# Strassen products of the feed-forward part in the order 1, 5, 7, 6, 2, 3, 4 instead of 1, 5, 6, 7, 3, 2, 4

## The chip, the cores and the metric

The kernel runs on one core of a Trainium2 chip. The metric is the device time of one execution in microseconds. TensorE (PE) multiplies, VectorE (DVE), ScalarE (ACT) and GpSimd (POOL) work element by element, SyncE (SP) issues most of the transfers, and each runs its own instruction queue in order; semaphores tie them together.

## The reference

One step of a decoder trunk. Three token mixers and their gates come first; the change touches only the feed-forward part behind them, with D = 1024, D_FF = 2816 and 1056 rows (1024 of the prompt, 32 of the samples):

```
x = x + (mixed @ w_out).astype(x.dtype)
h2 = rmsnorm(x, norm2_w)
gu = h2 @ w_ffn_up
x = x + ((jax.nn.silu(gu[..., :D_FF]) * gu[..., D_FF:]) @ w_ffn_down).astype(x.dtype)
...
y_prompt = rmsnorm(xp, final_norm_w)
y_sample = rmsnorm(xs, final_norm_w)
```

## The kernel before

Every operand of a matmul is split into a high and a low part, so that each product of tiles takes three matmuls (low times high, high times low, high times high: L2144, L2145, L2146). The mixers and the output projection fill the first 1005 us. From there on the feed-forward part runs as 37 "pairs" x, each a 2 by 2 block product done in Strassen-Winograd form with seven block products instead of eight. Pairs 0 to 20 (`UP_PAIRS` = 21) make the up projection: one pair gives one tile of the gate half and one of the value half for all 1056 columns, in two halves of 528 (`LOWER`, `UPPER`). Pairs 21 to 36 make the down projection: four groups d of 4, 6, 6 and 6 tiles of the inner dimension (`DOWN_TILES`), and in each group four pairs m. A product is 24 matmuls of 264 columns in an up pair, 12 in group 0 and 18 in groups 1 to 3.

**Accumulators.** Four pairs of PSUM banks ("quads") hold the products. Products 1, 5, 7 and 2 start a quad afresh; 6 is added onto 1 in the same quad, 3 onto 5, and 4 onto 7 (`QUAD`, `FRESH`). So product 6 may start only when 1 has been read out, 3 when 5 has, and 4 when 7 has. The rule for that is `bank_free` (L2105): it waits on counters of the reading engines.

**Readers, up pair.** ACT copies quad 1 to R1 (L2696) once product 1 is done, and the sum 1+6 to R2 (L2708). DVE then makes RV = R2 + 5, f upper = RV + 7, f lower = R2 + 3, RG = R1 + 2, RV = R2 + 4 ("quadrants", L3300 and below, counter `dr`), ACT applies SiLU to RG and RV (L2674), and DVE multiplies them in (`ffn_product`). Beside every odd pair the operands for the down projection are made of two finished f tiles: DVE forms four sums, ACT casts seven high parts (`f_high`, L2669), DVE subtracts seven low parts (`f_low`), and SP stores them in HBM (L1125).

**Readers, down pair.** DVE adds the quads straight onto X1 (`down_add`, counter `dd`): one add for product 1 and 5 each, three for 1+6, one for 7, 3, 2, 4 each, nine in all. In the last three pairs the squares of the final norm are added between them (`square_sum`).

**Weights.** SP loads the raw weights of a pair (`raw_load`), ACT casts the high part of each product's stationary operand into a ring of six slots (`weight_high`, L2643), POOL subtracts the low part (`low`) and overwrites the raw tiles with the four weight differences that later products need (`difference`; both are L1249). All queues are written out by hand in the order of the products. `ORDER[i]` is the product at position i, and `done_count` the value of the matmul counter when it is done. The operands of the down projection come back from HBM by `f_load`, one per product and group, into tiles that `F_AT` names.

Lines that matter here:

```python
ORDER, LAST_ORDER = (1, 5, 6, 7, 3, 2, 4), (1, 5, 6, 7, 4, 3, 2)
QUAD = {1: 0, 6: 0, 5: 2, 3: 2, 7: 4, 4: 4, 2: 6}
...
    after(act, pd, done_count(x, 1))
    if x >= 1:
        after(act, dr, 5 * x - 1)
    nc.scalar.copy(by_chunk(R1), quad(1)).then_inc(ar_used.sem, 1)
```

## Time and profile before

| what | us |
|---|---|
| median of 3 runs | 1741.16 |
| lowest and highest | 1740.33, 1742.37 |
| the profiled execution's own time | 1742.4 |
| its span, first to last instruction | 1740.7 |
| PE busy with matmuls | 1660.2 (95%) |
| ACT, DVE, POOL busy | 557.6, 951.8, 797.6 |
| up pairs 0 to 20 | 1013.2 to 1471.1 |
| down pairs 21 to 36 and final norm | 1471.1 to 1740.7 |

The profile is of one execution; its own time lies 1.2 us above the median and 1.7 us above its span. Mean granted clock of TensorE over the span: 0.989 of full speed. In the views below, a row of the timeline gives start, duration, engine, line, operation, output and inputs, and in brackets how long the engine had been idle before it and what released it. A row of the waits gives the total, the number and the longest of such waits.

### The profile page before, as it was taken

Reading aid. Unit: us, or ns where it says so; the run is one execution under the profiler, and the core shown is the slowest. Engines: PE = TensorE matmul, PEld = TensorE weight load, DVE = VectorE, ACT = ScalarE, POOL = GpSimd, SP = SyncE. Lnnn points to the kernel's source line nnn. Section 1 sums busy time; section 2 is a strip of 40 time slices with the busy share of each in tenths; the row PEclk is TensorE's granted clock in tenths of the full one; section 3 lists DMA queues with packets and bytes.
Section 4 is the critical chain, followed back from the end, with each engine's and each line's share of the span. In section 5 each row is a group of like instructions: output and inputs, shape, how many; then the busy total and the mean of one; then the engine's idle time right before and its main releaser. Section 6 shows DMA issues by size and latency. Waiting matters only on the chain.

```text
span 1740.7 us, 30849 instructions
## 1 busy us (share of the span) xinstructions
PE 1660.2 (95%) x12229; PEld 1605.7 (92%) x12229; DVE 951.8 (55%) x1615; ACT 557.6 (32%) x1239; POOL 797.6 (46%) x761
## 2 busy tenths in 40 slices
PE   7999999999999999999999969999999999889995
PEld 7999999999999998788999969999999998889994
DVE  6859711407345546869742575555555554724446
ACT  5332121432123324434210343334333433312232
POOL 5482122222221121323322357777777775757772
PEclk9999999999999999999999989999999999999998
DMA  5454463232323246243552503333343347877432
GB/s 202 87 120 133 124 188 99 88 89 85 96 91 99 86 141 196 87 148 124 198 183 86 197 25 137 136 136 136 136 136 136 137 161 289 315 278 274 181 140 100
DMA packets 94299, 252.36 MB, mean 145 GB/s; under 512 B 14528, under 2 KB 35008, under 8 KB 93912
## 3 DMA queue, kind: packets, MB, share of 16 engines
q1 hardware_dynamic: 72144, 180.98, 30.8%
q10 hardware_dynamic: 12056, 37.03, 6.2%
q0 software_dynamic: 9968, 32.54, 6.1%
q8 instruction: 90, 1.47, 0.3%
q14 instruction: 41, 0.34, 0.1%
HBM read 179.85 MB, written 70.44 MB: 144 GB/s over the span
## 4 chain that ended last, share of the span: by engine, by line
PE 75%; DVE 8%; POOL 7%; issue 4%; ACT 4%; DMA 2%; SPq 0%; ACTq 0%; DVEq 0%; POOLq 0%
PE ps L1559 14%; PE ps L1560 13%; PE ps L1561 13%; PE ps L2144 9%; PE ps L2146 9%; PE ps L2145 9%; POOL RAWB L1249 4%; DVE X L2789 1%; POOL WL L1249 1%; DMA x_scratch<-X 1%; POOL RINGB L1249 1%; POOL WH L1249 1%; ACT STG L2669 1%; PE ps L1989 1%; PE ps L2080 1%
## 5 line engine op out<-in xcount | busy, mean ns | idle before, releaser
L1559 PE MATMUL ps<-HL,WH 128*128 128x384 f32 x1488 | 492.3, 331 | 5.3 <-DVE HL L685 1.8
L1560 PE MATMUL ps<-HH,WL 128*128 128x384 f32 x1488 | 481.7, 324 | 0.0
L1561 PE MATMUL ps<-HH,WH 128*128 128x384 f32 x1488 | 481.1, 323 | 0.0
L1559 PEld LDWEIGHTS ps<-HL,WH 128*128 128x128 f32 x1488 | 280.6, 189 | 16.7 <-issue 9.3
L1560 PEld LDWEIGHTS ps<-HH,WL 128*128 128x128 f32 x1488 | 280.8, 189 | 0.3
L1561 PEld LDWEIGHTS ps<-HH,WH 128*128 128x128 f32 x1488 | 280.5, 188 | 0.0
L1224 POOL TENSOR_TENSOR WL<-WRAW,WH 128x1024 fp32r<-128x1024 f32 x59 | 145.1, 2459 | 233.8 <-DMA WH<-in_w 233.8
L2789 DVE TENSOR_TENSOR X<-X,ps 128x528 f32<-128x528 f32 (+1 forms) x162 | 107.2, 681 | 177.0 <-PE ps L2146 126.1
L1221 POOL DMA_DIRECT2D WH<-in_w x59 | 34.5, 585 | 364.8 <-PE ps L1561 363.2
L2201 ACT ACTIVATE GT<-ps 128x384 f32<-128x384 f32 (+1 forms) x72 | 33.3, 464 | 214.9 <-PE ps L1561 183.8
L1249 POOL TENSOR_TENSOR RAWB<-RAWB 128x512 f32<-128x512 f32 (+2 forms) x76 | 98.5, 1297 | 7.2
L2144 PE MATMUL ps<-SOP,WH 128*128 128x264 f32 x268 | 78.1, 292 | 19.9 <-ACT FS L2648 9.0
L1249 POOL TENSOR_TENSOR WRAW<-WRAW 128x512 f32<-128x512 f32 (+2 forms) x72 | 86.7, 1204 | 6.8
L2144 PE MATMUL ps<-HL,WH 128*128 128x264 f32 x304 | 86.3, 284 | 3.3 <-issue 3.3
L2789 DVE TENSOR_TENSOR RB<-RB,ps 128x528 f32<-128x528 f32 x63 | 44.0, 699 | 81.8 <-ACT RB L2708 51.4
L2144 PE MATMUL ps<-SOP,WL 128*128 128x264 f32 x270 | 78.0, 289 | 8.2 <-ACT RB L2696 7.3
L2145 PE MATMUL ps<-HH,WL 128*128 128x264 f32 x292 | 83.1, 285 | 0.0
L2146 PE MATMUL ps<-HH,WL 128*128 128x264 f32 x292 | 83.0, 284 | 0.0
L2145 PE MATMUL ps<-HH,RINGB 128*128 128x264 f32 x292 | 82.9, 284 | 0.0
L2146 PE MATMUL ps<-HH,RINGB 128*128 128x264 f32 x292 | 82.8, 284 | 0.0
L2144 PE MATMUL ps<-SOP,RINGB 128*128 128x264 f32 x254 | 72.9, 287 | 7.3 <-ACT RB L2696 3.7
L2145 PE MATMUL ps<-HH,WH 128*128 128x264 f32 x280 | 79.6, 284 | 0.0
(459 smaller groups left out, 4301.2 us busy)
## 6 DMA issues: line engine op xcount, KB each, us to landing
WRAW<-in_w SPq DMA_DIRECT2D x75, 512.0 KB, 3.3
ffn_scratch<-STG SPq DMA_DIRECT2D x70, 528.0 KB, 4.0
WH<-in_w POOLq DMA_DIRECT2D x60, 512.0 KB, 4.5
SOP<-ffn_scratch SPq DMA_DIRECT2D x36, 528.0 KB, 12.9
gate_scratch<-GT ACTq DMA_DIRECT2D x24, 528.0 KB, 3.5
HH<-ffn_scratch SPq DMA_DIRECT2D x24, 528.0 KB, 9.0
PX<-gate_scratch ACTq DMA_DIRECT2D x22, 528.0 KB, 4.0
RAWB<-in_w SPq DMA_DIRECT2D x11, 1024.0 KB, 5.0
```

The costliest lines, as they stand in the source:

```text
L1221: nc.gpsimd.dma_start(WH[:, slot, 0:wd], src[:, 0:wd]).then_inc(s_high[slot], 16)
L1224: nc.gpsimd.tensor_tensor(WL[:, slot, 0:wd], WRAW[:, slot, 0:wd], WH[:, slot, 0:wd].bitcast(F32), ALU.subtract).then_inc(split_ok, 1)
L1249: return nc.gpsimd.tensor_tensor(out, a, b, op)
L1559: nc.tensor.matmul(out, wh, rl, start=start, stop=False)
L1560: nc.tensor.matmul(out, wl, rh, start=False, stop=False)
L1561: return nc.tensor.matmul(out, wh, rh, start=False, stop=stop)
L1989: last = nc.tensor.matmul(bank[3 + kv][:, 256 * i + lo:256 * i + 256], blk(PU[r:r + 64, 4 + 2 * half + i, :], n), PX[r:r + 64, 6, P * (n - ...
L2144: nc.tensor.matmul(out, wh, ml, start=product in FRESH and k == 0, stop=False, skip_group_check=True)
L2145: nc.tensor.matmul(out, wl, mh, start=False, stop=False, skip_group_check=True)
L2146: last = nc.tensor.matmul(out, wh, mh, start=False, stop=k == nk - 1, skip_group_check=True)
L2201: nc.scalar.activation(GT[:, c0:c0 + w], acc_of(no, n)[:, 0:w], ACT.Tanh, scale=0.5).then_inc(acc_free[n], 1)
L2789: return nc.vector.tensor_tensor(out, a, b, op)
```

## The change

The order of the products becomes 1, 5, 7, 6, 2, 3, 4 in all pairs but the last, and 1, 5, 7, 6, 4, 3, 2 in the last. Products 6 and 7 change places, and so do 3 and 2. Everything that is written in the order of the products is moved along: the counts that TensorE waits for, the order of low parts and differences on POOL, of casts and copies on ACT, and of quadrants and adds on DVE. On ACT the cast for the next pair's first product now stands ahead of the R2 copy, and two casts of the down operands stand one weight cast earlier. The tiles of group 0 and 1 of the down operands are permuted, so that each load still goes into a tile that is free by then; each product still reads its own operand from the HBM scratch (`ROW_OF`). Nothing is added or removed: the number of matmuls, element-wise operations and transfers and their sizes stay the same.

```diff
@@ -66,7 +66,7 @@
 UP_PAIRS = DFF // P - 1
 DOWN_TILES = [4, 6, 6, 6]
 PAIRS = UP_PAIRS + 4 * len(DOWN_TILES)
-ORDER, LAST_ORDER = (1, 5, 6, 7, 3, 2, 4), (1, 5, 6, 7, 4, 3, 2)
+ORDER, LAST_ORDER = (1, 5, 7, 6, 2, 3, 4), (1, 5, 7, 6, 4, 3, 2)
 QUAD = {1: 0, 6: 0, 5: 2, 3: 2, 7: 4, 4: 4, 2: 6}
 FRESH = (1, 5, 7, 2)
 RING = 6
@@ -908,8 +908,8 @@
         return HH[:, i, :] if i < 8 else HL[:, i - 8, :] if i < 16 else SOP[:, i - 16, :]
 
     H0_, H1_, H2_, H3_, H4_, Q0_, Q1_, Q2_, Q3_ = (0, 3, 6, 9, 12, 16, 19, 22, 25)
-    F_AT = [[16, 18, 20, 22, 24, 26, 12], [H0_, H1_, H2_, H3_, Q0_, Q1_, Q2_], [Q3_, H4_, H0_, H1_, H2_, H3_, Q0_],
-            [Q1_, Q2_, Q3_, H4_, H0_, H1_, H2_]]
+    F_AT = [[16, 18, 24, 26, 20, 22, 12], [H0_, H1_, H2_, H3_, Q0_, Q3_, Q1_], [Q2_, H4_, H0_, H1_, H2_, H3_, Q0_],
+            [Q3_, Q1_, Q2_, H4_, H0_, H1_, H2_]]
     ROW_OF = {1: 0, 5: 1, 6: 2, 7: 3, 3: 4, 2: 5, 4: 6}
     F_FIRST = [0, 2, 5, 8]
 
@@ -925,7 +925,7 @@
         cols = slice(CHUNK * c, CHUNK * c + CHUNK)
         if x >= UP_PAIRS:
             d = (x - UP_PAIRS) // 4
-            t = f_tile(F_AT[d][ROW_OF[product]] + k)
+            t = f_tile(F_AT[d][ORDER.index(product)] + k)
             return t[:, LOWER][:, cols], t[:, UPPER][:, cols]
         if product in (5, 6, 7):
             return [a[:, k, cols] for a in s_rows(product - 5)]
@@ -1132,7 +1132,7 @@
             if freed is not None:
                 after(sp, pd, freed)
             for k in range(DOWN_TILES[d] // 2):
-                sp.dma_start(f_tile(F_AT[d][i] + k).bitcast(F32), fscr[F_FIRST[d] + k, i]).then_inc(s_fop[i].sem, 16)
+                sp.dma_start(f_tile(F_AT[d][i] + k).bitcast(F32), fscr[F_FIRST[d] + k, ROW_OF[ORDER[i]]]).then_inc(s_fop[i].sem, 16)
 
         for x in range(UP_PAIRS):
             q = f_pair_beside(x)
@@ -1151,9 +1151,9 @@
                 f_load(0, 1)
             raw_load(x + 2)
             if x == UP_PAIRS - 1:
-                f_load(0, 2, done_count(x, 6))
+                f_load(0, 2, done_count(x, 7))
                 f_load(0, 3)
-                f_load(0, 4, done_count(x, 7))
+                f_load(0, 4, done_count(x, 6))
                 f_load(0, 5)
                 f_load(0, 6, done_count(x, 4))
             if q is not None:
@@ -1174,7 +1174,7 @@
                 f_load(3, 4, done_count(x, ORDER[2]))
             if (d, m) == (0, 3):
                 f_load(1, 4, done_count(x, ORDER[1]))
-                f_load(1, 5, done_count(x, ORDER[2]))
+                f_load(1, 5, done_count(x, ORDER[3]))
             if x + 2 < PAIRS:
                 raw_load(x + 2)
             if (d, m) == (0, 1):
@@ -1537,10 +1537,11 @@
             difference(x, W12, W11, W11, 1, 0)
             difference(x, W22, W12, W12, 1, 1)
             low(x, 1)
+            low(x, 2)
             difference(x, W22, W11, W11, 2, 2)
-            low(x, 2)
-            difference(x, W21, W11, W11, 3, 3)
-            for i in range(3, 7):
+            low(x, 3)
+            difference(x, W21, W11, W11, 4, 3)
+            for i in range(4, 7):
                 low(x, i)
 
         for i, half in enumerate((UPPER, LOWER)):
@@ -2117,18 +2118,18 @@
                 if product in (5, 6, 7, 3):
                     after(pe, sl_ok, 4 * {5: 1, 6: 2, 7: 3, 3: 4}[product])
             elif x < UP_PAIRS:
-                after(pe, *{1: (ar_used, 2 * x), 6: (ar_used, 2 * x + 1), 5: (dr, 5 * x - 2), 3: (dr, 5 * x + 1),
-                             7: (dr, 5 * x), 4: (dr, 5 * x + 2), 2: (dr, 5 * x - 1)}[product])
+                after(pe, *{1: (ar_used, 2 * x), 6: (ar_used, 2 * x + 1), 5: (dr, 5 * x - 1), 3: (dr, 5 * x + 1),
+                             7: (dr, 5 * x), 4: (dr, 5 * x + 2), 2: (dr, 5 * x - 2)}[product])
             else:
                 y = 9 * (x - UP_PAIRS)
                 if y == 0 and product in (1, 5, 7, 2):
-                    after(pe, *{1: (ar_used, 2 * x), 5: (dr, 5 * x - 2), 7: (dr, 5 * x), 2: (dr, 5 * x - 1)}[product])
+                    after(pe, *{1: (ar_used, 2 * x), 5: (dr, 5 * x - 1), 7: (dr, 5 * x), 2: (dr, 5 * x - 2)}[product])
                 else:
-                    turn = {1: y - 4, 6: y + 1, 5: y - 2, 3: y + 2, 7: y, 4: y + 6, 2: y - 1}[product]
+                    turn = {1: y - 3, 6: y + 1, 5: y - 1, 3: y + 2, 7: y, 4: y + 3, 2: y - 2}[product]
                     after(pe, dd, turn)
                 if (x - UP_PAIRS) % 4 == 0:
                     d = (x - UP_PAIRS) // 4
-                    after(pe, s_fop[ROW_OF[product]], 8 * sum(DOWN_TILES[:d + 1]))
+                    after(pe, s_fop[ORDER.index(product)], 8 * sum(DOWN_TILES[:d + 1]))
 
         def strassen_product(x, i):
 
@@ -2692,7 +2693,7 @@
                 h_sum_high(3)
             after(act, pd, done_count(x, 1))
             if x >= 1:
-                after(act, dr, 5 * x - 1)
+                after(act, dr, 5 * x - 2)
             nc.scalar.copy(by_chunk(R1), quad(1)).then_inc(ar_used.sem, 1)
             if q is not None:
                 f_high(q, 0)
@@ -2702,23 +2703,22 @@
             weight_high(g + 6)
             if q is not None:
                 f_high(q, 2)
+            weight_high(g + 7)
             after(act, pd, done_count(x, 6))
             if x >= 1:
                 after(act, dr, 5 * x)
             nc.scalar.copy(by_chunk(R2), quad(6)).then_inc(ar_used.sem, 1)
             if q is not None:
                 f_high(q, 3)
-            weight_high(g + 7)
             weight_high(g + 8)
             if q is not None:
                 f_high(q, 4)
+                f_high(q, 5)
             weight_high(g + 9)
-            if q is not None:
-                f_high(q, 5)
-            silu(x, RG, 4)
-            weight_high(g + 10)
+            silu(x, RG, 3)
             if q is not None:
                 f_high(q, 6)
+            weight_high(g + 10)
         silu(UP_PAIRS - 1, RV, 5)
 
         def final_square(k, half, out, adds):
@@ -3357,10 +3357,11 @@
             if q is not None:
                 f_sum_last(q)
                 f_low(q, 4)
-            quadrant(x, f[:, LOWER], R2, 3, 2)
+            quadrant(x, RG, R1, 2, 2)
             if q is not None:
                 f_low(q, 5)
-            quadrant(x, RG, R1, 2, 3)
+            quadrant(x, f[:, LOWER], R2, 3, 3)
+            after(dve, dr, 5 * x + 4)
             ffn_product(x, LOWER, RG, 1)
             if q is not None:
                 f_low(q, 6)
@@ -3402,9 +3403,10 @@
                 after(dve, s_x1l[(0, 1, 1, 2)[m]], (32, 64, 64, 32)[m])
             down_add(x, m, 0, 0, 1)
             down_add(x, m, 1, 1, 5)
+            down_add(x, m, 1, 1, 7, 2)
             down_add(x, m, 0, 1, 6)
             down_add(x, m, 1, 0, 6)
-            down_add(x, m, 1, 1, 6, 2)
+            down_add(x, m, 1, 1, 6, 3)
             if x == UP_PAIRS:
                 f_sums(10)
             if x == UP_PAIRS + 1:
@@ -3418,25 +3420,24 @@
                 for j in range(2):
                     after(dve, fad, 2 * m - 3 + j)
                     square_sum(slice(0, T), (SQ5, GT)[j], 2 * m - 1 + j)
-            down_add(x, m, 1, 1, 7, 5)
             if x == PAIRS - 1:
                 break
-            down_add(x, m, 0, 1, 3, 3)
+            down_add(x, m, 0, 0, 2, 1)
             if x == UP_PAIRS:
                 f_low(10, 0)
                 f_low(10, 1)
-            down_add(x, m, 0, 0, 2, 1)
+            down_add(x, m, 0, 1, 3, 4)
             if x == UP_PAIRS + 1:
                 for i in range(4, 7):
                     f_low(10, i)
-            down_add(x, m, 1, 0, 4, 4)
+            down_add(x, m, 1, 0, 4, 5)
 
         after(dve, fad, 5)
         square_sum(UPPER, GT, 7)
-        down_add(x, m, 1, 0, 4, 4)
+        down_add(x, m, 1, 0, 4, 5)
         after(dve, fad, 6)
         square_sum(UPPER, SQ5, 8)
-        down_add(x, m, 0, 1, 3, 3)
+        down_add(x, m, 0, 1, 3, 4)
         square_sum(LOWER, GT, 9)
         final_recip(0)
         final_rows(0, (2,))
```

On ACT in pair 3, an odd one, from the R1 copy on (RB<-ps; the first is R1, the second R2; STG casts are `f_high`, the others `weight_high`); before:

```order
L2696 COPY RB<-ps 128x528
L2669 CAST STG<-GT 128x528
L2643 CAST WL<-WRAW 128x512
L2669 CAST STG<-SAB 128x528
L2643 CAST WL<-WRAW 128x512
L2669 CAST STG<-SAB 128x528
L2708 COPY RB<-ps 128x528
L2669 CAST STG<-GT 128x528
L2643 CAST RINGB<-RAWB 128x512 x2
L2669 CAST STG<-SAB 128x528
L2643 CAST WH<-RAWB 128x512
L2669 CAST STG<-FODD 128x528
```

and now:

```order
L2697 COPY RB<-ps 128x528
L2670 CAST STG<-GT 128x528
L2644 CAST WL<-WRAW 128x512
L2670 CAST STG<-SAB 128x528
L2644 CAST WL<-WRAW 128x512
L2670 CAST STG<-SAB 128x528
L2644 CAST RINGB<-RAWB 128x512
L2710 COPY RB<-ps 128x528
L2670 CAST STG<-GT 128x528
L2644 CAST RINGB<-RAWB 128x512
L2670 CAST STG<-SAB 128x528
L2670 CAST STG<-FODD 128x528
```

The first cast of the next pair (RINGB<-RAWB) moved ahead of the second copy, and the cast STG<-FODD moved ahead of the cast WH<-RAWB.

On POOL at the start of the feed-forward part, pair 0 (RAWB<-RAWB is a difference, the others are low parts of one product each); before:

```order
L1249 TENSOR_TENSOR RAWB<-RAWB 128x512 x2
L1249 TENSOR_TENSOR WH<-RAWB,WH 128x512
L1249 TENSOR_TENSOR RAWB<-RAWB 128x512
L1249 TENSOR_TENSOR WL<-RAWB,WL 128x512
L1249 TENSOR_TENSOR RAWB<-RAWB 128x512
L1249 TENSOR_TENSOR WL<-RAWB,WL 128x512
```

and now:

```order
L1249 TENSOR_TENSOR RAWB<-RAWB 128x512 x2
L1249 TENSOR_TENSOR WH<-RAWB,WH 128x512
L1249 TENSOR_TENSOR WL<-RAWB,WL 128x512
L1249 TENSOR_TENSOR RAWB<-RAWB 128x512
L1249 TENSOR_TENSOR WL<-RAWB,WL 128x512
L1249 TENSOR_TENSOR RAWB<-RAWB 128x512
```

The third difference, which product 6 needs, now stands behind the low part of product 7.

On DVE in the last pair, from the two full-width additions of squares on; before:

```order
L2789 TENSOR_TENSOR AC<-AC,SQ 128x1056
L2789 TENSOR_TENSOR AC<-AC,GT 128x1056
L2789 TENSOR_TENSOR X<-X,ps 128x528
L2789 TENSOR_TENSOR AC<-AC,GT 128x528
L2789 TENSOR_TENSOR X<-X,ps 128x528
L2789 TENSOR_TENSOR AC<-AC,SQ 128x528
```

and now:

```order
L2789 TENSOR_TENSOR AC<-AC,SQ 128x1056
L2789 TENSOR_TENSOR AC<-AC,GT 128x1056
L2789 TENSOR_TENSOR AC<-AC,GT 128x528
L2789 TENSOR_TENSOR X<-X,ps 128x528
L2789 TENSOR_TENSOR AC<-AC,SQ 128x528
```

The add of product 7 is gone from behind the two additions of squares; it stands ahead of the three adds of 1+6 now.

## Rows read from the trace of the kernel before

**Rows 1.** Waits of PE over the whole span: total, times, longest, in us.

```profile
PE ps L2144 <- ACT RB L2696: 13.9, 11, 4.4
...
PE ps L2144 <- ACT FS L2648: 9.0, 1, 9.0
```

**Rows 2.** Timeline of PE: first matmuls of products in pairs 2, 3 and 20.

```profile
1078.35 0.39 PE L2144 MATMUL ps<-SOP,RINGB 128*128 128x264 f32 x1 [0.92 <-ACT RB L2696]
...
1095.95 0.29 PE L2144 MATMUL ps<-SOP,RINGB 128*128 128x264 f32 x1
...
1101.79 0.28 PE L2144 MATMUL ps<-SOP,WH 128*128 128x264 f32 x1
...
1456.47 0.39 PE L2144 MATMUL ps<-SOP,RINGB 128*128 128x264 f32 x1 [0.95 <-ACT RB L2696]
```

**Rows 3.** Timeline of ACT in pairs 3 and 4.

```profile
1101.98 0.60 ACT L2708 COPY RB<-ps 128x528 f32<-128x528 f32 x1 [2.60 <-PE ps L2146]
...
1119.71 0.59 ACT L2696 COPY RB<-ps 128x528 f32<-128x528 f32 x1
```

**Rows 4.** Timeline of DVE in pair 3, the R2 copy's readers and the last drain.

```profile
1103.86 1.79 DVE L2789 TENSOR_TENSOR STG<-GT,STG 128x528 fp32r<-128x528 f32 x1
1105.74 0.70 DVE L2789 TENSOR_TENSOR GT<-RB,ps 128x528 f32<-128x528 f32 x1
...
1117.93 0.69 DVE L2789 TENSOR_TENSOR RB<-RB,ps 128x528 f32<-128x528 f32 x1
```

**Rows 5.** Timeline of PE in pair 0: products 5 and 6.

```profile
1025.29 0.59 PE L2144 MATMUL ps<-SOP,WH 128*128 128x264 f32 x1 [8.97 <-ACT FS L2648]
1034.34 0.59 PE L2144 MATMUL ps<-SOP,WL 128*128 128x264 f32 x1 [4.37 <-ACT RB L2696]
```

**Rows 6.** Timeline of ACT in pair 0.

```profile
1022.71 2.23 ACT L2656 CAST SOP<-X 128x528 fp32r<-128x528 f32 x4
1024.84 0.39 ACT L2648 ACTIVATE FS<-ps 128x288 f32<-128x288 f32 x1
```

**Rows 7.** Timeline of POOL in pair 0.

```profile
1022.36 2.34 POOL L1249 TENSOR_TENSOR WL<-RAWB,WL 128x512 fp32r<-128x512 f32 x1 [6.16 <-ACT WL L2643]
1024.78 1.27 POOL L1249 TENSOR_TENSOR RAWB<-RAWB 128x512 f32<-128x512 f32 x1
```

**Rows 8.** Timeline of DVE in pair 0: four operations of 528 columns.

```profile
1030.57 2.55 DVE L2789 TENSOR_TENSOR X<-X 128x528 f32<-128x528 f32 x4
```

**Rows 9.** Timeline of DVE in pair 20: the last subtraction for pair 19's operands.

```profile
1452.74 1.38 DVE L2789 TENSOR_TENSOR STG<-FODD,STG 128x528 fp32r<-128x528 f32 x1 [0.34 <-ACT STG L2669]
```

**Rows 10.** Timeline of SP's queue at pairs 20, 21 and 23.

```profile
1457.62 1.74 SPq L1128 DMA_DIRECT2D X<-x_scratch  x4
...
1506.01 4.49 SPq L1135 DMA_DIRECT2D HH<-ffn_scratch  x8
```

**Rows 11.** One stretch: us, busy of PE, PEld, DVE, ACT, POOL; clock, DMA share, GB/s.

```profile
1476.00:1478.00 2.00, 1.69 (x12) 1.51 (x12) 0.06 (x1) 0.00 (x0) 0.00 (x0) 1.00 1.01 414
```

**Rows 12.** Timeline of PE: last product of pair 21, one of pair 23, product 4 of pair 36.

```profile
1486.66 0.36 PE L2144 MATMUL ps<-HL,WL 128*128 128x264 f32 x1 [0.81 <-DVE X L2789]
...
1504.00 0.39 PE L2144 MATMUL ps<-SOP,WH 128*128 128x264 f32 x1 [1.09 <-DVE X L2789]
...
1712.57 0.39 PE L2144 MATMUL ps<-HH,RINGB 128*128 128x264 f32 x1 [2.90 <-DVE X L2789]
```

**Rows 13.** Timeline of DVE in pair 36.

```profile
1707.51 1.93 DVE L2789 TENSOR_TENSOR X<-X,ps 128x528 f32<-128x528 f32 x3 [1.49 <-PE ps L2146]
1709.36 1.25 DVE L2789 TENSOR_TENSOR AC<-AC,SQ 128x1056 f32<-128x1056 f32 x1
...
1716.56 0.71 DVE L2789 TENSOR_TENSOR AC<-AC,SQ 128x528 f32<-128x528 f32 x1 [0.78 <-ACT SQ L2727]
```

**Rows 14.** Timeline of PE: the sums over squares in the final norm.

```profile
1717.41 1.13 PE L2156 MATMUL ps<-AC,PRM 128*128 128x264 f32 x4 [0.18 <-DVE AC L2789]
...
1725.54 2.13 PE L2156 MATMUL ps<-SQ,PRM 128*128 128x264 f32 x4 [3.93 <-ACT SQ L2727]
```

## The prediction

> **What bounds the kernel now.** TensorE is busy 95% of the span, so the first view to read is what it waits for, and only then the queues that release it. The waits of PE [rows 1] show one that recurs: 11 times, 13.9 us in all, for ACT's R1 copy (L2696). One of them is 4.4 us long, which leaves ten of 0.95. The timeline of PE [rows 2] places these ten: product 6 of every even up pair from pair 2 to pair 20, evenly spaced, (1456.47 - 1078.35) / 9 = 42.01 us apart. A product without a stall takes (1101.79 - 1095.95) / 2 = 2.92 us [rows 2], 14 of them 40.88, so one such stall costs 42.01 - 40.88 = 1.13 us with the slow restart. The reason stands on ACT [rows 3]: product 5 of pair 4 is over at about 1119.3, but the R1 copy starts only at 1119.71, behind a weight cast that stands behind the SiLU of the odd pair's last drain, which DVE makes as late as 1117.93 [rows 4]. Product 6 has one product (5) between itself and product 1, which is 2.92 us for the copy, and that is not enough after an odd pair.
>
> The other idle time of PE has three places: pair 0 [rows 5], pairs 21 to 25 [rows 9 to 12], and the last pair [rows 12 to 14]. The pairs 26 to 35 show none.
>
> **Up pairs 2 to 20.** Let T be the start of an odd pair, with PE never waiting: products 1, 5, 7, 6, 2, 3, 4 start at T, 2.92, 5.84, 8.76, 11.68, 14.60, 17.52, and the even pair at 20.44. For pair 3 of the trace T is 1095.95 - 2.92 = 1093.03 [rows 2]. I go through what each product now waits for.
> - 6 waits for the R1 copy with two products between. In the trace that copy ends 1120.30 - 1093.03 = T + 27.3; product 6 of the even pair now starts at 20.44 + 8.76 = 29.2. The stall is gone, with 1.9 us to spare even if nothing ahead of the copy gets earlier.
> - 3 waits for the drain of 5, which follows the R2 copy. The copy can start at T + 11.7 now (8.8 to 8.9 before), the drain ends 1.3 us later, at 13.1; product 3 needs it at 14.6. Spare 1.5.
> - 4 waits for the drain of 7. In the trace it ended 1106.44 - 1101.98 = 4.5 us after the R2 copy began [rows 3, 4], so T + 16.2; needed at 17.5. Spare 1.3. This is the tightest place. It is open whether the two low-part subtractions between (one of them 1.79 us, with POOL running beside it [rows 4]; 2.55 / 4 = 0.64 without [rows 8]) both become slow: then T + 17.3, still in time.
> - 7 of the even pair waits for the drain of 4. It ended at 1118.62 - 1093.03 = T + 25.6 [rows 4] and is needed at 20.44 + 5.84 = 26.3. Spare 0.7 by the old times. I expect it nearer to T + 23, since the cast STG<-FODD no longer stands behind a cast that waits for a POOL difference.
> - 5 of the even pair waits for the drain of 3, one drain earlier in the queue, at T + 23.4. The weights: POOL starts on the next pair at T + 7 instead of T + 10.7, so its low parts are ready earlier, not later.
>
> So all ten stalls go. Nine of them lie ahead of pair 20 and count in full: 9 x 1.13 = **10.2 us**. The tenth lies in pair 20 and is in the term for pair 21.
>
> On the tight place, one rule of the skill. The trace shows a subtraction with two SBUF inputs at 1.79 us beside POOL work and at 0.64 without [rows 4, 8]. The Trainium skill, SBUF — State Buffer, section "Who interferes with whom", says that such a VectorE operation and a GpSimd one that reads SBUF exclude each other, the second waiting for the whole of the first. By that each of the two subtractions could take one POOL operation (1.27 [rows 7]) plus 0.64 = 1.9, the drain of 7 would end at T + 17.5 to 17.6, and the sum would lose at most 1 us over ten pairs; by the rows alone it loses nothing. The sum above goes by the rows.
>
> **Pair 0.** This part first loses. The cast for position 3 belongs to product 6 now and waits for the third difference, which POOL makes behind the low part of product 7: that low part ran to 1024.7, the difference takes 1.27 [rows 7], so ACT is held until 1026.05. Four casts (2.23) and the SiLU (0.39) stand behind it [rows 6], and product 5 waits for that SiLU [rows 5]: it starts at 1029.2 instead of 1025.29, 3.9 us late. Then it gains. DVE needs twice 2.55 us [rows 8], up to 1.3 more for POOL beside it, so the fourth sum is ready at about 1035.5 to 1036, its casts and the R1 copy at 1037.3. Meanwhile PE runs 5 (at the lower clock at first: the trace's product 5, also after an idle stretch, took 4.7 us with the row's first matmul at 0.59) until about 1034, then 7, whose operand is ready at 1033, until 1037 to 1038, and 6 begins without a break at about 1037.5. Before, 6 began at 1034.34, after 4.37 us of idle time, and ran at the lower clock again; pair 1 then started at 1078.35 - 1.13 - 5.84 - 20.44 = 1050.9 [rows 2]. Now 6, 2, 3, 4 follow at full clock: 1037.5 + 4 x 2.92 = 1049.2. Gain 1.7 to 2.5, taken as **2.0 us**; bounds: a loss of 1 (if 7 has to wait for its operand and the clock falls) and a gain of 3.
>
> **Pairs 20 and 21.** Here PE waits for down operands. In the stretch 1476 to 1478 the DMA moves 414 GB/s [rows 11]; two tiles of 528 KB take 2 x 0.541 / 414 = 2.6 us, which is the spacing of the products of pair 21, and its last one starts at 1486.66 [rows 12]. (The view names DVE there, but that add had long been made for the quad that matters.) This stream begins with the loads at 1457.62 [rows 10], and those wait for the last stores of pair 19's operands. Pair 20 starts at 1456.47 - 1.13 - 5.84 = 1449.50 and pair 19 at 1429.06; its last subtraction ends at 1452.74 + 1.38 = 1454.12 [rows 9], T + 25.1, in the trace and by my chain at T + 22.6, so the stream starts 2.4 to 2.5 us earlier against pair 20. Gain **2.4 us** (bounds 0.5 and 3; the stall of pair 20 is contained in it).
>
> **Pairs 22 to 25.** Here the change costs. Sums and subtractions of the last operands stand on DVE behind the three adds of 1+6, which now come one product (1.46 us in this group, half of 2.92) later; one add (about 0.6) less stands among them. In pair 23 product 7 at position 2 waits for pair 22's last add, where before 6 at position 2 waited the same way [rows 12]. The operands' stores and POOL's low parts release the next stream of loads, at 1506.01 [rows 10], and that one sets the pace until pair 25. Late by 1.46 - 0.6 = 0.9 at least, and by 2.1 if POOL's low parts of pair 23, which are held up by the same sums through ACT, come last. I take **1.8 us lost** (bounds 0 and 3). Pairs 26 to 35 have two products, 4.4 us, for a drain of 0.7 and nine adds in 15.3 us: nothing lost.
>
> **The last pair.** Product 4 waited 2.90 us there [rows 12], since the add of 7 stood behind two additions of squares. This wait goes, but I give it no gain: the end hangs on DVE and ACT. The three adds of 1+6 (1707.51 to 1709.4) come a product, 2.19 us, later. Then the two additions (2 x 1.25), then square 0.65 and addition 0.7 of tile 7, the add of product 4, again square and addition. By these durations the last of them ends at 1717.65, against 1716.56 + 0.71 = 1717.27 in the trace [rows 13]: **0.4 us lost**. And PE now idles from 1713.9 to 1717.8 in front of the first sum over squares. After the idle stretch of 3.93 us the sum took 2.13 us at the lower clock, without one 1.13 [rows 14]: **1.0 us lost**, or 0 if the clock holds.
>
> **Sum.** -10.2 - 2.0 - 2.4 + 1.8 + 0.4 + 1.0 = -11.4 us. Against the profiled execution: span 1740.7 to 1729.3, its own time 1742.4 to 1731.0. That execution lies 1.2 us above the median of the runs; from the median, 1741.16 - 11.4 = **1729.8 us**.
>
> **Rivals.**
> - The pair-0 loss is not paid back. The 3.9 us are certain; the gain depends on 7 finding its operand at once. If it waits and 6 starts cold as before, +3.9 stands in place of -2.0: 1735.7. For it: the operand is ready only 1 us ahead. Against it: DVE is idle while the SiLU is awaited.
> - DVE is late for product 4 in odd pairs. With an average of 0.3 us in ten pairs, 3 us less gain: 1732.8. If a subtraction waits for a second POOL operation (1.3 more), the drain ends at T + 18.6, the stall is 1.1 and takes up the whole gain: 1740.8.
> - Slower: product 7 of an even pair becomes the new waiter, for the drain of 4. It decides from T + 26.3. The distance was 8.8 us from 4's end with 7 at position 3 and is 5.8 now. If the drain ends 3 us later than in the trace, at T + 28.6, the stall is 2.3 us, ten times 23 us: -11.4 + 23 = +11.6, 1752.8. For it: the chain R2, quadrants, casts, SiLU now starts 2.9 us later after T. Against it: in the trace the chain had a hole of some 3 us for the POOL difference, and this is gone.
> - The order is changed but some count still asks for the later event, so that 6 waits as before: 1741.2.
>
> **How the numbers follow.** Forecast 0.70; late for 4 in part 0.11 (1732.8); pair 0 unpaid 0.11 (1735.7); gain eaten up or no effect 0.04 (1741); slower 0.04 (1753). Within the forecast the bounds of the terms, added as independent, give about 3 up and 4 down, so the range runs from 1725.5 to 1735.5 and leaves out the last two and part of the third. What a measurement of this kernel tells from no change is about 0.2%, 3.5 us; so faster 0.92, the same 0.04, slower 0.04.
>
> **What would show it.** In the profile after, the wait for L2697 (the R1 copy) is gone from PE's list, and the odd pairs start 40.9 us apart. Pair 0: product 5 starts at 1029, pair 1 at 1049. Pair 20 starts at 1437.3, the last product of pair 21 at 1472. The last pair has no wait for product 4 but one of about 4 us ahead of L2156. Wrong would be the sum if PE waited anew for DVE's RB or FODD in up pairs, at a spacing of 42 us, or if pair 1 started after 1052.

## The result

The changed kernel takes 1725.34 us (median of 4 runs, 1723.57 to 1726.25), the kernel before in the same comparison 1741.76 us (4 runs, 1740.33 to 1742.88). The ratio is 0.9905, 95% interval 0.9888 to 0.9922, so 16.4 us gained where 11.4 were forecast. The time lies 0.2 us below the forecast's range. A repeat beside other runs gave 1726.91 against 1740.88 (0.9923, 0.9909 to 0.9936), 14.0 us. The profiled execution's own time is 1723.57 us, its span 1721.8.

What PE waited for in the changed kernel, over the whole span (total, times, longest, in us); these lines answer to [rows 1]:

```profile
PE ps L2145 <- issue: 10.8, 6, 4.3
PE ps L2145 <- ACT FS L2649: 9.7, 1, 9.7
...
PE ps L2145 <- DVE X L2789: 6.6, 4, 1.8
PE ps L2157 <- DVE AC L2789: 3.8, 1, 3.8
...
PE ps L2157 <- ACT SQ L2727: 2.6, 1, 2.6
```

The wait for the R1 copy, 13.9 us and first in [rows 1], is gone, and no new wait in the up pairs has come for it. The first line, "issue", is idle time for which the profile names no releaser: 3.3 us ahead of pair 0, three stretches in pair 21 and two in pair 25. The other lines are the SiLU of pair 0, the down operands of pairs 21 to 25, and the final norm.

I cut the span at the starts of products, read from the timeline of PE, and did the same with a second profile of each kernel (runs e0 and e11 below). Times in us; "measured" is the difference of the two means:

| stretch | before, two profiles | after, two profiles | forecast | measured |
|---|---|---|---|---|
| up to pair 0 | 1013.2, 1011.1 | 1011.9, 1012.2 | 0 | -0.1 |
| pair 0 | 37.9, 37.4 | 34.9, 34.9 | -2.0 | -2.8 |
| pairs 1 to 19 | 398.5, 398.6 | 387.5, 387.5 | -10.2 | -11.0 |
| pairs 20, 21 | 38.7, 38.4 | 35.9, 36.4 | -2.4 | -2.4 |
| pairs 22 to 25 | 58.4, 57.9 | 58.3, 58.7 | +1.8 | +0.3 |
| pairs 26 to 35 | 154.1, 154.7 | 153.8, 153.3 | 0 | -0.9 |
| pair 36 to the end | 40.0, 40.0 | 39.7, 40.4 | +1.4 | 0.0 |
| span | 1740.7, 1738.2 | 1721.8, 1723.4 | -11.4 | -16.8 |

The last column rests on two executions of each kernel. The medians, of 4 to 9 executions, differ by less, 16.4 and 14.0 us. Pairs 1 to 19 repeat to 0.1 us; pairs 20 to 25 do not, as the repeats below show.

### The profile page after: what moved, and what is told of

Same layout as the page of the kernel before. It is cut to its first block, busy times and chain, and to the rows that moved or that the text cites. A ratio compares the mean times of both kernels' runs of the same rounds, so it can differ in the third digit from the quotient of the medians.

```text
span 1721.8 us, 30870 instructions
## 1 busy us (share of the span) xinstructions
PE 1657.1 (96%) x12229; PEld 1605.9 (93%) x12229; DVE 966.5 (56%) x1615; ACT 558.8 (32%) x1239; POOL 799.4 (46%) x761
## 4 chain that ended last, share of the span: by engine, by line
PE 86%; DVE 6%; issue 3%; ACT 2%; DMA 1%; POOL 1%; SPq 0%; DVEq 0%; ACTq 0%; POOLq 0%
PE ps L1560 14%; PE ps L1561 13%; PE ps L1562 13%; PE ps L2145 13%; PE ps L2147 13%; PE ps L2146 12%; DMA x_scratch<-X 1%; PE ps L1990 1%; PE ps L2081 1%; PE ps L1760 1%; PE ps L1734 1%; ACT SB L2499 1%; DVE X L2789 1%; PE ps L2054 1%; PE ps L1754 0%
## 5 line engine op out<-in xcount | busy, mean ns | idle before, releaser
L2202 ACT ACTIVATE GT<-ps 128x384 f32<-128x384 f32 (+1 forms) x72 | 33.3, 464 | 215.5 <-PE ps L1562 177.5
L2146 PE MATMUL ps<-HH,WH 128*128 128x264 f32 x280 | 81.3, 290 | 0.0
L2147 PE MATMUL ps<-HH,WH 128*128 128x264 f32 x280 | 81.1, 290 | 0.0
## 6 DMA issues: line engine op xcount, KB each, us to landing
SOP<-ffn_scratch SPq DMA_DIRECT2D x36, 528.0 KB, 13.1
```

Source lines behind the costliest of these rows:

```text
L2146: nc.tensor.matmul(out, wl, mh, start=False, stop=False, skip_group_check=True)
L2147: last = nc.tensor.matmul(out, wh, mh, start=False, stop=k == nk - 1, skip_group_check=True)
L2202: nc.scalar.activation(GT[:, c0:c0 + w], acc_of(no, n)[:, 0:w], ACT.Tanh, scale=0.5).then_inc(acc_free[n], 1)
```

## The experiments

**The stall by itself (e1).** The kernel before, with only this on ACT in even pairs from 2 on:

```diff
+            early = x >= 2 and x % 2 == 0
+            if early:
+                after(act, pd, done_count(x, 1))
+                after(act, dr, 5 * x - 1)
+                nc.scalar.copy(by_chunk(R1), quad(1)).then_inc(ar_used.sem, 1)
             silu(x - 1, RV, 5)
```

(the copy is taken out of its old place in these pairs).

> The kernel before, its product order untouched. In the ten even up pairs with f work beside them ScalarE takes the copy of product 1's bank ahead of the SiLU and the weight cast, not behind them, so the idle 1.1 us in front of product 6 should go without any new order of the products. Theory (the ten idles are the copy's lateness and nothing else): no wait of TensorE on the R1 copy above the one of pair 0, nine pairs each shorter by 42.01 - 40.79 = 1.22 us, the tenth (pair 20) worth nothing because the next pair is held by the f store and loads; 1741.8 - 11.0 = 1730.8 us. The other parts of the change (pair 0, pairs 20 and 21, the end) are not in it: pair 0 stays at 37.9 us and pairs 20/21 at 37.1 us. Rival (the old order has no slack on the other side: the SiLU or the cast that is now late stops TensorE at product 4, or at product 1 of the next pair): the idle comes back there, the gain is 4 us or less, 1737 to 1742 us.

Measured 1731.22 us (0.9935, 0.9918 to 0.9951), where the theory had 1730.8. The waits of PE:

```profile
PE ps L2144 <- ACT FS L2648: 9.0, 1, 9.0
PE ps L2144 <- DVE X L2795: 8.4, 5, 2.9
...
PE ps L2144 <- ACT RB L2702: 4.3, 1, 4.3
```

One wait for the R1 copy is left, pair 0's. Starts of pair 1 and of pair 20 on PE:

```profile
1051.24 0.28 PE L2144 MATMUL ps<-HL,WH 128*128 128x264 f32 x1
...
1438.77 0.28 PE L2144 MATMUL ps<-HL,WL 128*128 128x264 f32 x1
```

That is 387.5 us for pairs 1 to 19, the same as in the changed kernel, with the old order of products. Pair 0 (38.0) and pairs 20 and 21 (38.9) stayed. So the late copy is the whole of the 11.0 us of these pairs: the new order removes the wait by giving the copy more time, and a change of ACT's order alone does it too. The tenth stall was worth nothing by itself, as said in advance.

**Why 2 and 3 change places as well (e2).** The changed kernel with 3 ahead of 2 again:

```diff
-ORDER, LAST_ORDER = (1, 5, 7, 6, 2, 3, 4), (1, 5, 7, 6, 4, 3, 2)
+ORDER, LAST_ORDER = (1, 5, 7, 6, 3, 2, 4), (1, 5, 7, 6, 4, 3, 2)
```

(counts, quadrants and adds to match).

> The changed kernel with the order 1, 5, 7, 6, 3, 2, 4: product 7 ahead of 6 as in the change, but products 3 and 2 as before. Tells what the second exchange (2 ahead of 3) does. Theory (it is needed, because product 3 writes the bank of product 5, whose drain waits behind the copy of product 6, and with 6 right ahead of 3 nothing covers the two): TensorE waits ahead of product 3 for a drain of VectorE in each of the 21 up pairs, 1.3 to 1.6 us each, +27 to +34 us on the changed kernel's 1725.3: 1752 to 1760 us, slower than the kernel before. Rival (VectorE drains product 5 early enough): no wait ahead of product 3, within 3 us of 1725.3.

Measured 1759.6 us (1.0099, 1.0078 to 1.0121), with this wait of PE:

```profile
PE ps L2145 <- DVE RB L2789: 30.0, 21, 1.4
```

Once in each up pair PE waits for the drain of product 5, as the theory said. Exchanging 6 and 7 without exchanging 3 and 2 costs 34 us against the changed kernel, so the second exchange is what makes the first one pay. The exchange of 3 and 2 alone was not run.

**Pair 0 (e3, e4).** In the changed kernel the third difference holds ACT's cast, and product 5 waits for the SiLU behind it. ACT, then PE:

```profile
1024.09 0.62 ACT L2644 CAST WL<-RAWB 128x512 fp32r<-128x512 f32 x1 [3.74 <-POOL RAWB L1249]
...
1026.74 0.40 ACT L2649 ACTIVATE FS<-ps 128x288 f32<-128x288 f32 x1
```

```profile
1027.20 0.59 PE L2145 MATMUL ps<-SOP,WH 128*128 128x264 f32 x1 [9.72 <-ACT FS L2649]
```

e4 puts this cast behind the SiLU, e3 puts the SiLU ahead of that cast and of the four casts (`h_sum_high(2)`) too:

```diff
-        weight_high(3)
         h_sum_high(2)
         first_silu(2)
+        weight_high(3)
```

```diff
         first_silu(1)
+        first_silu(2)
...
-        first_silu(2)
```

> The changed kernel, with ScalarE's fourth weight cast of pair 0 (whose raw difference GpSimd now makes later than before) put behind the sum's cast and the SiLU that product 5 waits for. The prediction took 3.9 us of delay for product 5 from this wait and a gain of 2.0 us for pair 0 in spite of it; the trace showed 3.2 us and a gain of 3.0 us. Theory (the wait for GpSimd is the whole delay of product 5, and what follows it is not bound by it alone): product 5 of pair 0 starts 3 to 3.7 us earlier than in the changed kernel, at 11.6 to 12.3 us from product 1, and pair 1 starts 1 to 3 us earlier: 1722.3 to 1724.3 us. Rival (pair 0 is held at products 7 and 6 by the f sums and weight parts anyway, so that an earlier product 5 leaves a longer idle behind it): pair 0 keeps its 34.9 us, 1725.3 us.

> The changed kernel, with one step of ScalarE moved: in pair 0 the SiLU that product 5 waits for is taken as soon as the first one of its kind is done, ahead of two casts. It takes away the largest idle that is left in TensorE, 9.72 us ahead of product 5 of pair 0. Theory (only ScalarE's own order holds the SiLU back): product 5 starts 5 us or more earlier and pair 1 starts 2 to 4 us earlier, as the rest of pair 0 meets its own weights and sums: 1721.5 to 1723.5 us. Rival (the gated tile that it reads comes late itself, from VectorE, so the SiLU waits in its new place and the casts behind it with it): product 5 starts where it did or later, pair 1 up to 3 us later, 1725 to 1728.5 us.

e4: 1725.67 us (0.9911, 0.9893 to 0.993), no gain over the changed kernel that its median shows, where 1722.3 to 1724.3 had been expected; e3: 1730.18 us (0.9924, 0.9905 to 0.9943), slower. Products 5, 7 and 6 of pair 0 on PE in e4:

```profile
1023.89 0.59 PE L2145 MATMUL ps<-SOP,WH 128*128 128x264 f32 x1 [7.82 <-ACT FS L2649]
1029.90 0.36 PE L2145 MATMUL ps<-SOP,WL 128*128 128x264 f32 x1 [0.82 <-DVE SOP L2789]
1034.42 0.39 PE L2145 MATMUL ps<-SOP,WL 128*128 128x264 f32 x1 [1.38 <-ACT RB L2697]
```

Product 1 had started at 1012.91, so 5 came at +11.0 (us behind the start of product 1), 4.4 us earlier than in the changed kernel (+15.3), 0.7 more than expected. Products 7 and 6 then waited for their own inputs, and pair 0 shrank only by 1.6 us, to 33.3. In e3 product 5 ran at +4.4, and 7 waited 11.4 us, here on PE and on DVE:

```profile
1032.82 0.56 PE L2145 MATMUL ps<-SOP,WL 128*128 128x264 f32 x1 [11.41 <-DVE SOP L2789]
```

```profile
1027.29 5.27 DVE L2789 TENSOR_TENSOR SOP<-X,SOP 128x528 fp32r<-128x528 f32 x4 [3.35 <-ACT SOP L2657]
```

Pair 0 took 36.4 us, 1.6 longer than without the edit, though product 5 stood 11.0 us earlier. Neither the theory nor the rival for e3 held. The SiLU came early, and then product 7 had to wait for its low parts, which stand behind ACT's casts, and those behind the same POOL difference as in the changed kernel. But this wait is not what made pair 0 longer: 7 started at +19.0, 1.1 us earlier than in the changed kernel (+20.1), and the R1 copy ended 0.6 us earlier. What was lost is the clock. One stretch inside product 7, first in e3, then in the changed kernel (us; busy of PE, PEld, DVE, ACT, POOL; clock, DMA share, GB/s):

```profile
1033.00:1038.00 5.00, 5.00 (x23) 5.00 (x24) 4.51 (x8) 4.49 (x8) 1.20 (x1) 0.50 0.00 0
```

```profile
1032.00:1034.90 2.90, 2.90 (x25) 2.80 (x24) 2.90 (x6) 2.90 (x6) 0.00 (x0) 1.00 0.00 0
```

In e3 PE had been idle for 11.4 us ahead of product 7, the granted clock was 0.50 (the lower of its two levels, 1.2 GHz), and 7 took 5.4 us. In the changed kernel 7 followed product 5 without a break, at 1.00, and took 3.0 us.

**The loads of the last down operands (e5, e8).** On the queue of SP in pairs 22 and 23 of the changed kernel:

```profile
1485.17 1.53 SPq L1128 DMA_DIRECT2D X<-x_scratch  x2
1488.47 0.90 SPq L1104 DMA_DIRECT2D WRAW<-in_w  x2
1489.46 4.78 SPq L1135 DMA_DIRECT2D HH<-ffn_scratch  x8
```

Against the start of pair 22 (1470.12 us; before, 1488.20) the loads HH are 1.5 us later, 19.3 for 17.8 us [rows 10]. The prediction had expected that and put +1.8 us on it. e8 moves the two loads of x behind the raw loads, so that they no longer fill the time:

```diff
             if (d, m) == (0, 1):
                 for i in range(2, 7):
                     f_store(10, i)
-                for j in (6, 7):
-                    x1_load(j)
             if (d, m) == (0, 2):
+                for j in (6, 7):
+                    x1_load(j)
                 after(sp, s_fsl, 16 * 7)
```

e5 makes the last store earlier instead:

```diff
+            if x == UP_PAIRS + 1:
+                for i in range(4, 7):
+                    f_low(10, i)
             down_add(x, m, 0, 0, 2, 1)
...
             down_add(x, m, 0, 1, 3, 4)
-            if x == UP_PAIRS + 1:
-                for i in range(4, 7):
-                    f_low(10, i)
```

> The changed kernel; on SyncE's queue in pairs 22 and 23 the two loads of x (1.08 MB) stand behind the raw weight loads, not ahead of them. In the changed kernel the raw loads and the f loads behind them are issued 1.8 and 1.5 us later against pair 22 than before, at 18.35 and 19.34 us, and pairs 22 to 25 cost the same. Theory (the two loads of x kept the transfer engines full until then, so the later issue was hidden): with the cover gone the engines idle for 1.5 to 3 us between the last store and the raw loads, and pairs 22 to 25 take that much longer, 60 to 61.5 us instead of 58.3 to 58.8; 1727 to 1729.5 us. Rival (something later sets the pace of pairs 24 and 25, and the issue never mattered): 58.2 to 58.9 us, 1725 to 1727 us.

> The changed kernel; in pair 22 VectorE takes the last three low parts of the f sums ahead of the adds of products 2 and 3, not behind them, so that the last f store, and the loads of x and of the next f rows that follow it on SyncE's queue, are issued about 1.2 us earlier. The prediction put +1.8 us on this stretch because these parts became later; the trace showed 0. Theory (the loads' stream is full up to the product that waits for it, and begins with the last store): pairs 22 to 25 are 0.5 to 1.2 us shorter than in the changed kernel (58.3 us), 1724.1 to 1724.8 us. Rival (the stream is limited by something else, the two raw loads or GpSimd's low parts ahead of them): 58.3 us again, or up to 0.7 us more where products of pair 23 now wait for the two adds.

e8: 1728.77 us (0.9924, 0.9907 to 0.9942). The stretch from 14 to 20 us behind the start of pair 22 (columns as above), first in the changed kernel, then in e8:

```profile
1484.12:1486.12 2.00, 0.67 (x5) 0.67 (x6) 2.00 (x4) 1.02 (x3) 1.33 (x3) 1.00 1.04 420
1486.12:1488.12 2.00, 2.00 (x19) 2.00 (x18) 1.21 (x2) 0.71 (x2) 2.00 (x4) 1.00 0.99 302
1488.12:1490.12 2.00, 2.00 (x19) 2.00 (x18) 1.43 (x3) 0.05 (x1) 1.78 (x4) 1.00 0.99 370
```

```profile
1485.75:1487.75 2.00, 0.67 (x4) 0.67 (x5) 2.00 (x4) 1.02 (x3) 1.33 (x3) 0.94 1.04 420
1487.75:1489.75 2.00, 2.00 (x11) 2.00 (x10) 0.50 (x1) 0.71 (x2) 2.00 (x4) 0.50 0.55 222
1489.75:1491.75 2.00, 2.00 (x14) 2.00 (x13) 0.70 (x1) 0.08 (x1) 1.78 (x4) 0.71 0.18 58
```

In the changed kernel the transfer engines are busy without a hole, as they are in the kernel before at this place (0.99 to 1.04); in e8 the share falls to 0.55 and 0.18, 2.5 us of transfer time lost, and pairs 22 to 25 take 60.7 us for 58.3 and 58.7. So the later issue is real and was hidden by the loads of x. The edit does one thing more: the loads HH now stand behind those of x and are issued 1.0 us later still (20.3 us). The 60.7 lies only 0.5 us above the longest of this stretch without the edit (see e5); what carries the reading is the hole in the share. The clock fell to 0.50 in e8 as well; this is not the cause, since e10 below had 0.65 and 0.50 in the same place with a full DMA share, and took 57.6:

```profile
1484.10:1486.10 2.00, 2.00 (x12) 2.00 (x13) 1.03 (x2) 0.98 (x3) 1.48 (x3) 0.65 1.04 418
1486.10:1488.10 2.00, 2.00 (x11) 2.00 (x10) 0.70 (x1) 0.71 (x2) 2.00 (x3) 0.50 1.01 279
```

e5: 1726.84 us (0.9923, 0.9909 to 0.9937). The loads of x were issued at 13.5 for 15.1 us against pair 22, but the raw loads, held by POOL's low parts, at 18.1 for 18.4. Pairs 22 to 25 took 58.2 us. That is within the scatter of this stretch (58.2 to 60.2 in seven profiles with the changed kernel's instructions there: after, e0, e3, e4, e6, e7, e9), so e5 by itself tells nothing; e5 and e10 together, 58.2 and 57.6 against a mean of 59.0, lean to the theory and do not show it.

**The end (e6, e7).** The final norm has three sums over squares on PE. The first and the last of them, in the changed kernel and then in its repeat e0:

```profile
1699.27 1.33 PE L2157 MATMUL ps<-AC,PRM 128*128 128x264 f32 x4 [3.77 <-DVE AC L2789]
...
1707.59 1.16 PE L2157 MATMUL ps<-SQ,PRM 128*128 128x264 f32 x4 [2.56 <-ACT SQ L2727]
```

```profile
1700.13 2.10 PE L2157 MATMUL ps<-AC,PRM 128*128 128x264 f32 x4 [3.77 <-DVE AC L2789]
...
1709.22 1.17 PE L2157 MATMUL ps<-SQ,PRM 128*128 128x264 f32 x4 [3.33 <-ACT SQ L2727]
```

e6 and e7 are, on PE (both) and on DVE (e7; there ACT also takes the last square and the second root ahead of the first spread copy):

```diff
-        for i in range(6):
+        for i in range(7):
             strassen_product(PAIRS - 1, i)
...
         final_sum(1, UPPER, AC5, True, True).then_inc(fsum.sem, 1)
-        strassen_product(PAIRS - 1, 6)
```

```diff
         down_add(x, m, 0, 1, 3, 4)
+        down_add(x, m, 0, 0, 2, 1)
         square_sum(LOWER, GT, 9)
         final_recip(0)
-        final_rows(0, (2,))
-        down_add(x, m, 0, 0, 2, 1)
-        final_rows(0, (3, 4, 5, 6))
+        final_rows(0, (2, 3, 4, 5, 6))
```

> The changed kernel; in the last pair TensorE takes product 2 ahead of the first sum over the squares, not behind it. The sum waits 3.77 us for VectorE there; product 2 (2.2 us) fits in. Tests the term of the prediction that charged 1.0 us for the lowered clock after this wait. Theory (the clock falls in the wait, and the first sum pays for it): the wait is 1.5 us, the sum takes 1.13 us as in the kernel before, not 1.33 to 1.6, and the last pair is 0.2 to 0.5 us shorter than 39.66: 39.2 to 39.5 us. Rival (the clock costs the chain nothing in the new order, because the first reciprocal and product 2 cover it): 39.6 to 39.7 us.

> The kernel of the run before this one, and also: VectorE adds product 2 in the 0.7 us in which it waits for ScalarE's last square but one, not between the rows of the end, and ScalarE takes the last square and the second root ahead of the copy of the first reciprocal. Theory (VectorE's own work from the first reciprocal on sets the end: 3.47 + 3.47 + twelve rows of 0.69, one add of 0.62 and one wait of 0.67): the add goes from that chain, the last pair is 0.6 us shorter than in the run before, 38.6 to 39.0 us. Rival (the outputs' DMAs set the end, as 4.3 MB leave in the last 13 us): no more than 0.2 us.

e6: 1725.55 us (0.992, 0.9906 to 0.9933), last pair 40.4 us, longer than the theory (39.2 to 39.5) and the rival (39.6 to 39.7) said. All three sums:

```profile
1700.05 1.13 PE L2157 MATMUL ps<-AC,PRM 128*128 128x264 f32 x4 [1.59 <-DVE AC L2788]
1702.09 1.13 PE L2157 MATMUL ps<-AC,PRM 128*128 128x264 f32 x4 [0.90 <-DVE AC L2788]
1708.17 2.13 PE L2157 MATMUL ps<-SQ,PRM 128*128 128x264 f32 x4 [4.95 <-ACT SQ L2726]
```

The first sum took 1.13 us as I had said, but the gain I expected is not there: PE now idles 4.95 us ahead of the last sum, and that one takes 2.13. That is how the kernel before behaved [rows 14]. The granted clock within the sums goes with these durations: 1.00 and 1.13 us (first sum of the kernel before), 0.80 and 1.33 (first sum of the changed kernel), 0.50 and 2.10 to 2.13 (first sum of e0, last sums of e6 and of the kernel before).

The length of the last pair can be added up from this. From the end of the first sum to the start of the last it is 7.0 us, and from the end of the last sum to the end of the kernel 13.0 us, in every profile but those with e7's edit. So each microsecond that either sum loses to the clock is a microsecond of the last pair. It is not always paid once: in e3 and e8 the first sum took 2.10 us and the last one 1.79 and 1.72, and the last pair 41.1 and 41.0 us.

In e7 (1725.75 us; 0.9918, 0.9904 to 0.9932) the last sum follows the middle one at once and both are fast. The last pair takes 38.8 us, within the 38.6 to 39.0 of the theory, but 1.6 us below e6 and not 0.6: the edit also took away the last sum's slow clock (1.05 us for 2.13), which I had not counted. The median shows nothing of the gain. In the profiled execution pairs 20 to 25 took 97.7 us, against 95.1 and 95.5 in those of e0 and e6; whether that is so in the other executions is not shown.

**Repeats and the two edits together (e0, e11, e9, e10).** e9 is e4 and e7 in one kernel, e10 is e9 and e5.

> The changed kernel once more, for a second profile beside the next three and for the spread of stretches that no instruction of the change lies in. What is to be told apart: which terms of the 16.4 us come again. Theory: pair 0 34.9 us, pairs 1 to 19 387.5 us, last pair 39.7 us, each within 0.2; pairs 20 and 21 with the loads behind them move with the DMA traffic: 35.9 us in the first profile of the changed kernel, 37.3 and 37.7 in two variants whose instructions there are the same, so about 37 here, and the gain of 2.8 us read there is rather 1 to 2. Rival: 35.9 again, and the variants' edits in pair 0 reach that far. Time 1723 to 1727 us.

> The kernel before once more, for a second profile. It tells which stretches of the difference between the two first profiles (18.9 us, where the medians differ by 14.0 to 16.4) come again. Theory: pair 0 37.9 us, pairs 1 to 19 398.5 us, last pair 40.0 us, each within 0.2; in pairs 20 and 21 the last product of pair 21 starts 28.8 to 29.7 us after the issue of the loads of x, and that issue is 2.8 to 5 us after the last subtraction, as it waits for a store to land: 38.0 to 40.0 us. Rival: stretches without DMA differ by over 0.5 us too.

> The changed kernel with the two edits that shortened a stretch in their own profiles: ScalarE's fourth cast of pair 0 behind the SiLU, and the last pair with product 2 ahead of the first sum, its add ahead of the first reciprocal and the last square ahead of the first copy. Theory (the two stretches do not touch each other): pair 0 takes 33.3 us and the last pair 38.8 us, together 1.6 + 1.4 = 3.0 us less than in the changed kernel's repeat (34.86 and 40.40); the two stretches that hang on the landing of stores differ by up to 2 us from one profile to the next, so 1722.5 to 1725 us beside 1725.3 to 1726.9. Rival (the stores' landing takes the gain of pair 0 back, since the stream starts no earlier): 1724.5 to 1726.5 us.

> The kernel of the run before this one with the three low parts of pair 22 ahead of the adds of products 2 and 3 too, which by itself took about 0.5 us from product 4 of pair 25 against pair 22 and nothing measurable from the time. Theory (the last store then lands earlier, and the stream with it): pairs 22 to 25 0.3 to 0.6 us shorter than in the run before, the time within 1 us of it. Rival (the two adds hold up products of pair 23 by as much): the same.

The changed kernel again (e0) gave 34.9 and 387.5 us as expected, but 40.4 us for the last pair and not 39.7: its first sum took 2.10 us, not 1.33. The kernel before again: 1741.0 us (ratio to its other runs 1.0001, 0.9992 to 1.001). Pair 0 was 0.5 us shorter there than expected, and pairs 26 to 35 0.6 longer, so the theory that only the stretches with transfers vary did not hold. In pairs 20 and 21 one step varies that no instruction explains. Queue of SP in the changed kernel, and in e9 with the same instructions there:

```profile
1434.48 2.66 SPq L1125 DMA_DIRECT2D ffn_scratch<-STG  x2
1439.64 1.74 SPq L1128 DMA_DIRECT2D X<-x_scratch  x4
```

```profile
1432.35 2.66 SPq L1125 DMA_DIRECT2D ffn_scratch<-STG  x2
1439.58 1.74 SPq L1128 DMA_DIRECT2D X<-x_scratch  x4
```

The last store (the second of the row) is issued 2.6 us after the start of pair 20 in both, the loads of x, which wait for it to land, 5.4 and 7.5 us after it. The last product of pair 21 comes 28.7 to 30.1 us behind these loads in all fourteen profiles. So the stretch takes 35.9 to 38.4 us in ten profiles of the new order that differ nowhere in it, mean 37.1, against 38.7, 38.9 and 38.4 in the old one. Why the stores land in two groups of times is open; no run was made on it.

e9: 1724.43 us (0.9898, 0.9882 to 0.9913), pair 0 33.3, last pair 38.8; it lost part of it to pairs 20 and 21, 38.4 us. e10: 1722.34 us, the fastest kernel here, 3.0 us below the changed one; its interval (0.9889, 0.9872 to 0.9906) overlaps with that of the changed kernel's first comparison and lies just below that of its repeat. That it is faster rests on pair 0 (33.3) and the last pair (38.8) as much as on the median.

## Why the prediction was right and wrong

The direction and the mechanism of the largest term were right. The forecast lay 4.5 us above the median because several terms were mis-sized in one direction: +1.8 for the late issue in pairs 22 to 25 (measured +0.3), +1.4 for the last pair (0.0), -2.0 for pair 0 (-2.8), -10.2 for the stalls (-11.0), and nothing for pairs 26 to 35 (-0.9). The repeat, 1726.91 us and 14.0 us of gain, would have been inside the range.

- **Up pairs: right in mechanism, 0.8 us too small.** In pair 3 of the changed kernel (T = 1046.71 + 2 x 20.39 = 1087.5) the three places I had called tight are, on DVE:

```profile
1099.98 0.70 DVE L2789 TENSOR_TENSOR RB<-RB,ps 128x528 f32<-128x528 f32 x1 [2.35 <-ACT RB L2710]
1100.60 0.70 DVE L2789 TENSOR_TENSOR STG<-SAB,STG 128x528 fp32r<-128x528 f32 x1
1101.22 1.80 DVE L2789 TENSOR_TENSOR STG<-GT,STG 128x528 fp32r<-128x528 f32 x1
1103.11 0.70 DVE L2789 TENSOR_TENSOR GT<-RB,ps 128x528 f32<-128x528 f32 x1
...
1110.35 0.69 DVE L2789 TENSOR_TENSOR RB<-RB,ps 128x528 f32<-128x528 f32 x1
```

  and on POOL beside them:

```profile
1101.08 1.38 POOL L1249 TENSOR_TENSOR RINGB<-RAWB,RINGB 128x512 fp32r<-128x512 f32 x1 [0.86 <-ACT RINGB L2644]
```

  The drain of 5 ends at T + 13.2 (forecast 13.1), of 7 at T + 16.3 (16.2), of 4 at T + 23.5 (23). Of the two subtractions between the drains of 5 and 7 one was slow, 1.80 us, the other took 0.70. POOL ran one instruction beside them, which began when the first subtraction was all but over, so only the second met it. By the Trainium skill, SBUF — State Buffer, section "Who interferes with whom", a VectorE instruction with two SBUF inputs contends with a GpSimd one that reads SBUF; the trace agrees with that here (1.80 us beside the POOL instruction, 0.70 without), and the case in which both are slow did not come. What failed is the price of a stall: I took a product as 2.92 us from one pair of rows. Over 133 products it is 387.5 / 133 = 2.914, so a stall is 42.01 - 14 x 2.914 = 1.22 us and nine are 11.0.
- **Pair 0: right sign, 0.8 to 1.0 us too small.** The delay of product 5 was 3.2 us (+15.3 for +12.1), not 3.9. The step that failed is "6 begins at about 1037.5", 24.35 us from product 1: it began at +23.1 and without idle time. I had put the fourth sum at +22.4 to +22.9 and the end of the R1 copy at +24.2; they came at +21.9 and +23.0. Most of this is the 0.7 us by which product 5 was less late, and the rows show where that comes from. The eight sums on DVE that stand ahead of all this, in the kernel before and in the changed one:

```profile
1015.44 5.65 DVE L2789 TENSOR_TENSOR X<-X 128x528 f32<-128x528 f32 x8
```

```profile
1014.14 5.03 DVE L2789 TENSOR_TENSOR X<-X 128x528 f32<-128x528 f32 x8
```

  In the kernel before POOL made the third difference (1.64 us) beside them; now it stands later, and they are 0.6 us shorter, in every profile of either order. I had let the change delay the difference without asking what it had held up in its old place. The rest is the tail behind the fourth sum, which I put at 1.3 to 1.8 us and which takes 1.2 in both kernels. The DVE work behind product 5 took as long as I had allowed with POOL beside it.
- **Pairs 20 and 21: right on the profiles (-2.4), luck in part.** The last subtraction came earlier, by 2.0 us (the start of pair 20 + 2.6 us, for 4.6 before) where 2.4 to 2.5 were worked out; the stream follows it by a distance that varies by 2 us. The mean of ten profiles of the new order against three of the old gives -1.5.
- **Pairs 22 to 25: wrong.** The step that failed is taking the later issue of the loads as time lost. The issue slipped by 1.5 us as said, but I had priced it without asking what the transfer engines did until then: their share was 0.99 to 1.04, and e8 shows a hole as soon as the cover is moved away. Two profiles of either kernel give +0.3; the seven against three of the old order (with e1) give +0.7, with a scatter of 2 us.
- **Pairs 26 to 35: -0.9 not forecast.** They took 154.1 to 154.7 us in the old order, in the new mostly 153.3 to 153.9, 154.4 in e10. The scatter lies in one step of up to 0.6 us in pair 29 or 33, which some profiles have, and in pair 26, which takes 15.3 us when the clock is back at 1.00 by its start (e0) and up to 16.0 when it is not (the kernel before: 0.58 in its first microsecond), as PE waits 3.4 to 4.3 us ahead of the last product of pair 25; pair 35 takes 15.5 in the old order and 15.3 in the new. Why the two orders should differ in this is open.
- **The last pair: wrong by 1.4.** The first sum started 0.4 us later as forecast. The step that failed is the 1.0 us for the clock: it was charged to the first sum (it took 1.33 to 2.10 us for 1.13) without taking back what the last sum had paid before, 2.13 in [rows 14], 1.16 and 1.17 now. With the fixed distances above that gives +0.4 + 0.2 - 1.0 = -0.4 in the first profile and +0.4 + 1.0 - 1.0 = +0.4 in the second, which is what the last pair shows (39.7 and 40.4 for 40.0). The mean of 0.0 is no sign that the clock costs nothing.

No rival came true. The range was also not what its terms give: their bounds, added as independent, are 2.4 us of gain and 3.7 of loss, not 4 and 3, and the stalls and pairs 26 to 35 had none.

## What to carry to other kernels

A stall that returns with every iteration is settled by one look at who is queued ahead of the releasing instruction: here one copy moved on ScalarE is worth the same 11 us as the new order of products. An issue that came 1.5 us later cost nothing here while the DMA share stayed near 1, so look at the share between the old and the new issue before pricing it. When a change moves an idle stretch of TensorE, list every stretch and what the clock costs behind each, before and after: here one cost came and another went, and in e3 an earlier product left a longer idle stretch and a slower pair. And when an instruction is moved, ask what it had been holding up in its old place.
